# Weights of the second mixer split once, during the first; query and gate columns in one unit; softmax moved ahead of value sums

## The reference

```
# layer 1, mixer A (chunked gMLP), width 2048
h  = rms_norm(x, a_norm) * (1 + scale) + shift          # shift, scale, gate from c
u, v, z = split(h @ a_w_in)                             # (1024 x 6144)
v  = layer_norm(gelu(v)); mixed = per group lower-triangular 128x128 of v in chunks of 128
x  = x + gate * ((gelu(u) * mixed * silu(z)) @ a_w_out)
# shared keys and values
kv = rms_norm(x, kv_norm) @ w_kv;  k = rope(k)
# layer 2, mixer B (sliding window 128, 16 query heads, 2 key heads, sinks)
h  = rms_norm(x, b_norm) * (1 + scale) + shift
q, z = split(h @ b_w_in)                                # (1024 x 2048)
o  = softmax([q k^T / 8 masked, sink]) @ v              # blocks of 128 queries, 256 keys
x  = x + gate * ((o * silu(z)) @ b_w_out)
out = rms_norm(x, final_norm)
```

## Time and profile before

| | us |
|---|---|
| median of 3 runs | 2423.5 (2421.96 to 2425.0) |
| profiled execution, its own time | 2430.8 |
| its span, first to last instruction | 2429.0 |
| PE (matmul) busy in the span | 2274.2 (94%) |
| PE weight load busy | 1899.4 (78%) |
| DVE / POOL / ACT busy | 1314.8 / 1116.1 / 947.8 |
| granted TensorE clock, mean | 0.977 |
| moved by DMA | 375.73 MB, mean 155 GB/s |

### The profile page before, as it was taken

The page is one execution under the profiler, slowest core; times in us unless marked ns, Lnnn a source line. Parts: engine busy times, 40 slices in busy tenths (PEclk is TensorE's granted clock), DMA queues, the critical chain, the costliest instruction groups (busy, mean ns, idle before and its releaser), DMA issues.

```text
span 2429.0 us, 28242 instructions
## 1 busy us (share of the span) xinstructions
PE 2274.2 (94%) x10725; PEld 1899.4 (78%) x10725; DVE 1314.8 (54%) x1767; ACT 947.8 (39%) x1730; POOL 1116.1 (46%) x646
## 2 busy tenths in 40 slices
PE   3999999999999999999999999969789989998898
PEld 2787878888888888888888888857767877787786
DVE  5647891315744315644414554266577577657854
ACT  3223233433333433333423333344445545445553
POOL 3345554444444344444444443424544555564554
PEclk9999999999999999999999999989899999999999
DMA  7753334433434333344333346473634464573433
GB/s 278 268 202 114 128 130 165 165 97 120 147 113 169 128 119 117 121 144 156 121 104 105 122 140 224 134 251 102 237 106 159 176 239 132 187 256 130 156 113 113
DMA packets 188327, 375.73 MB, mean 155 GB/s; under 512 B 14272, under 2 KB 85024, under 8 KB 187552
## 3 DMA queue, kind: packets, MB, share of 16 engines
q1 hardware_dynamic: 185760, 368.65, 44.3%
q10 hardware_dynamic: 2432, 5.28, 0.6%
HBM read 295.23 MB, written 69.21 MB: 150 GB/s over the span
## 4 chain that ended last, share of the span: by engine, by line
PE 76%; DVE 10%; DMA 5%; DVEq 2%; issue 2%; ACT 2%; POOL 1%; SPq 1%; POOLq 0%; ACTq 0%
PE ps L1461 23%; PE ps L1463 23%; PE ps L1462 23%; PE ps L1611 2%; DMA w_raw<-in_a_w_out 1%; DMA r<-b_input 1%; PE ps L1649 1%; PE ps L1650 1%; POOL w_lo L704 1%; DVE wh L1305 1%; DVEq L1404 1%; DVE y_hl L1259 1%; DVE qs L1375 1%; DMA w_raw<-in_b_w_in 1%; PE ps L1673 1%
## 5 line engine op out<-in xcount | busy, mean ns | idle before, releaser
L704 POOL TENSOR_TENSOR w_lo<-w_raw,w_hi 128x1024 fp32r<-128x1024 f32 x360 | 900.9, 2513 | 991.1 <-ACT w_hi L814 990.7
L814 ACT ACTIVATE w_hi<-w_raw 128x1024 fp32r<-128x1024 f32 x360 | 380.3, 1061 | 822.6 <-DMA w_raw<-in_a_w_in 519.0
L1461 PE MATMUL ps<-h,w_hi 128*128 128x512 f32 x1024 | 402.3, 393 | 0.0
L1462 PE MATMUL ps<-h,w_hi 128*128 128x512 f32 x1024 | 398.9, 390 | 0.0
L1463 PE MATMUL ps<-h,w_lo 128*128 128x512 f32 x1024 | 398.8, 389 | 0.0
L1461 PE MATMUL ps<-r,w_hi 128*128 128x512 f32 x512 | 212.9, 416 | 26.8 <-DMA r<-b_input 11.3
L1463 PEld LDWEIGHTS ps<-h,w_lo 128*128 128x128 f32 x1024 | 192.5, 188 | 40.6
L1462 PEld LDWEIGHTS ps<-h,w_hi 128*128 128x128 f32 x1024 | 192.6, 188 | 39.5 <-issue 0.2
L1461 PEld LDWEIGHTS ps<-h,w_hi 128*128 128x128 f32 x1024 | 192.6, 188 | 39.2 <-POOL w_lo L704 0.2
L1462 PE MATMUL ps<-r,w_hi 128*128 128x512 f32 x512 | 206.1, 403 | 0.0
L1463 PE MATMUL ps<-r,w_lo 128*128 128x512 f32 x512 | 206.1, 402 | 0.0
(11 more groups left out here) (200 smaller groups left out, 4093.1 us busy)
## 6 DMA issues: line engine op xcount, KB each, us to landing
w_raw<-in_a_w_in SPq DMA_DIRECT2D x256, 256.0 KB, 3.0
w_raw<-in_a_w_in SPq DMA_DIRECT2D x64, 512.0 KB, 4.7
w_raw<-in_a_w_out SPq DMA_DIRECT2D x64, 512.0 KB, 4.1
w_raw<-in_b_w_in SPq DMA_DIRECT2D x64, 512.0 KB, 4.6
kv_input<-xks SPq DMA_DIRECT2D x32, 512.0 KB, 5.7
b_input<-hbs SPq DMA_DIRECT2D x32, 512.0 KB, 6.5
r<-b_input SPq DMA_DIRECT2D x16, 1024.0 KB, 10.9
w_raw<-b_out_gated SPq DMA_DIRECT2D x32, 512.0 KB, 4.2
```

The lines of the kernel that those rows point to most:

```text
L704: g.tensor_tensor(wlo[p][:, rows_], raw[p][:, rows_], whi[p][:, rows_].bitcast(F32), ALU.subtract).then_inc(w_lo, 1)
L814: s_.activation(whi[p][:, rows_], raw[p][:, rows_], ACT.Copy).then_inc(w_hi, 1)
L1461: t_.matmul(dst_, stat[0], mov[0], start=start, stop=False)
L1462: t_.matmul(dst_, stat[0], mov[1], start=False, stop=False)
```

## The change

- **Splitting.** The 13 distinct weight units of kv and B (26 halves, `SPLIT_UNITS`) are split once while A runs, in the stages `SPLIT_STAGES`: stages 6 to 10 of each group and 1, 2 of groups 1 to 3 (0 to 3 are value stages, 4 to 11 are u and z). In stage q SP loads the half into `wsr` ahead of the stage's odd unit; ACT copies it to `wsh` and POOL subtracts into `wsl` after the w_hi and w_lo of the next odd unit; SP stores both (512 KB each) to `b_weights_split` one stage later (`keep_split`). For the output weights (the last eight) DVE multiplies by the gate first; POOL's products L752 and their loads and stores go.
- **B's weights.** `b_half` loads `w_hi` and `w_lo` directly, two DMAs of 512 KB per half, and `hi` and `lo` are not called in B. PE waits for the landing.
- **Units of B.** q and z units are replaced by `qz` units of 256 query and 256 gate columns, n = 0 to 3. The order is kv, 8 qz units, 4 b units of the group before. Query tiles are in banks 0 and 1, gate tiles in 2 and 3.
- **Slots.** 6 before the first step, and 5 to 7 pieces in each step's slot.
- **Softmax order.** The gated output of step a is done by DVE in slot a + 2 after piece 0, behind that slot's softmax, instead of in slot a + 1 after piece 3. `oz_round` and `oz_rest` move behind piece 1 and 2.
- **First inputs.** Half of B's inputs of group 0 (`hb0`, 2 MB) are loaded into the place of `y_hl[0]` during A's last output units; PE waits for the quarters of `r` one by one.
- **Last group's tiles** use four banks, 4 to 7; the first logits wait for the sixth, the first transposes of probabilities for the eighth.

```diff
+    for i in range(NG):
+        units.append(("kv", i, 0, 0))
+        for n in range(4):
+            for ku in range(2):
+                units.append(("qz", i, n, ku))
         if i >= 1:
             for n in range(2):
                 for ku in range(2):
                     units.append(("b", i - 1, n, ku))
...
-PRO_SLOTS, STEPS, TAIL_SLOTS = 8, 16, 7
+PRO_SLOTS, STEPS, TAIL_SLOTS = 6, 16, 7
...
-    edges = [8 * n - 8 for n in B_STARTS[1:NG + 1]] + [8 * B_STARTS[NG + 1] + 4, B_PIECES]
+    edges = [30, 118, 208, 308, B_PIECES - 28, B_PIECES]
...
+SPLIT_UNITS = [("kv", 0, 0)] + [("qz", n, ku) for n in range(4) for ku in range(2)] \
+    + [("b", n, ku) for n in range(2) for ku in range(2)]
+SPLIT_STAGES = [(i, q) for i in range(NG) for q in ((1, 2) if i else ()) + (6, 7, 8, 9, 10)]
...
             def b_half(u, hh):
+                for m, w in ((0, whi[p]), (1, wlo[p])):
+                    sp.dma_start(w[:, 2 * hh:2 * hh + 2].bitcast(F32), wsd[split_of(u, hh), m]) \
+                        .then_inc(raw_in[2 * p + hh], 16)
...
+            def load_split(s):
+                if s >= 2:
+                    sp.wait_ge(split_out[m], 32 * (s // 2))
...
+            def keep_split(s):
+                sp.wait_ge(split_lo, s + 1)
+                sp.dma_start(wsd[s, 0], wsh[s % 2][:].bitcast(F32)).then_inc(split_out[s % 2], 16)
+                sp.dma_start(wsd[s, 1], wsl[s % 2][:].bitcast(F32)).then_inc(split_out[s % 2], 16)
+
+            def a_stage(i, q):
+                if q >= 1:
+                    unit(first + 2 * q)
+                s = split_at(i, q)
+                if s is not None:
+                    load_split(s)
+                if q >= 1:
+                    unit(first + 2 * q + 1)
+                s = split_at(i, q - 1)
+                if s is not None:
+                    keep_split(s)
...
                 for g in range(GROUPS + 1):
-                    unit(first + U_UZ + 2 * g)
-                    unit(first + U_UZ + 2 * g + 1)
+                    a_stage(i, 4 + g)
                     if i >= 1 and g >= 2:
                         keep_turned(i - 1, g - 2)
...
+            def split(i, q):                     # POOL; ACT has its like
+                pool.wait_ge(split_hi, s + 1)
+                g.tensor_tensor(wsl[m][:], wsr[m][:], wsh[m][:].bitcast(F32), ALU.subtract).then_inc(split_lo, 1)
...
                 for n in range(3, 10):
                     lo(first + n)
+                    if n % 2 == 1:
+                        split(i, (n - 3) // 2)
...
-                for u, hh in weights_at(pc):
-                    lo(u, (hh,))
...
-                    pe.wait_ge(w_lo, 2 * u + hh + 1)
+                    pe.wait_ge(raw_in[2 * (u % 2) + hh], landed(u))
...
-                        if 0 <= a - 2 < ATT and (a - 2) % 4 == 3:
-                            oz_rest(a - 2)
+                        if 0 <= a - 2 < ATT:
+                            gated_output(a - 2)
...
-                        x1_transposes(NG - 1, kt, 4 + kt % 2)
+                        x1_transposes(NG - 1, kt, 4 + kt % 4)
```

More of the change, by code:

```diff
@@ L43, in b_order @@
 def b_order():
[L46 to L50, removed]
+    units = []
+    for i in range(NG):
+        units.append(("kv", i, 0, 0))
+        for n in range(4):
             for ku in range(2):
[L52 to L60, removed]
+                units.append(("qz", i, n, ku))
         if i >= 1:
@@ L70, in b_order @@
             units.append(("b", NG - 1, n, ku))
-    return units, starts + [len(units)]
-B_UNITS, B_STARTS = b_order()
+    return units
+B_UNITS = b_order()
 B_AT = {unit: ub for ub, unit in enumerate(B_UNITS)}
@@ L121, in order, with split_at, splits_by, split_landed @@
     return (k % 4, k // 4) if by_halves(u) else (k // 2, k % 2)
[L124 to L134, removed]
+SPLIT_UNITS = [("kv", 0, 0)] + [("qz", n, ku) for n in range(4) for ku in range(2)] \
+    + [("b", n, ku) for n in range(2) for ku in range(2)]
+SPLITS = 2 * len(SPLIT_UNITS)
+SPLIT_STAGES = [(i, q) for i in range(NG) for q in ((1, 2) if i else ()) + (6, 7, 8, 9, 10)]
+FIRST_GATED = 2 * SPLIT_UNITS.index(("b", 0, 0))
+def split_at(i, q):
+    return SPLIT_STAGES.index((i, q)) if (i, q) in SPLIT_STAGES else None
+def splits_by(i, m):
+    return sum(1 for s, (g, _) in enumerate(SPLIT_STAGES) if g <= i and s % 2 == m)
+def split_landed(s):
+    return 16 * sum(2 if SPLIT_UNITS[t // 2][0] == "qz" else 1 for t in range(s % 2, s + 1, 2))
+def split_of(u, hh):
+    kind, g, n, ku = B_UNITS[u - FIRST_B]
+    return 2 * SPLIT_UNITS.index((kind, n, ku)) + hh
 def turned_at(pc):
     return (pc - 8) // 3 if pc >= 8 and pc % 3 == 2 and pc < 8 + 3 * KT else None
[L142 to L149 removed]
+def column_at(pc):
+    kind, g, n, ku, k = unit_of(pc)
+    if kind in ("qz", "b") and ku == 1:
+        if by_halves(FIRST_B + pc // 8):
+            return (kind, g, n, k - 4) if k >= 4 else (None, 0, 0, 0)
+        return (kind, g, n, k // 2) if k % 2 == 1 else (None, 0, 0, 0)
+    return None, 0, 0, 0
+def query_at(pc):
+    kind, g, n, j = column_at(pc)
+    return (g, 2 * n + j) if kind == "qz" and j < 2 else None
+def gate_at(pc):
+    kind, g, n, j = column_at(pc)
+    return (g, 2 * n + j - 2) if kind == "qz" and j >= 2 else None
+def gates_at(pc):
+    return [gate_at(last) for last in (pc - 1, pc) if gate_at(last) and (last % 8 == 7) == (last == pc)]
 def keys_in(s):
@@ L430, in landed @@
         def landed(u):
-            return 16 * sum(2 if w < FIRST_B and U_UZ <= w % A_UNITS < U_AO else 1 for w in range(u % 2, u + 1, 2))
+            return 16 * sum(2 if w >= FIRST_B or U_UZ <= w % A_UNITS < U_AO else 1 for w in range(u % 2, u + 1, 2))
         @block.sync
@@ L547, in _ @@
                 for j in range(4):
-                    if j >= 1:
-                        unit(first + 2 * j)
-                        unit(first + 2 * j + 1)
+                    a_stage(i, j)
                     if i == 0:
@@ L588, in _ @@
                             load_xk(0, part)
+                    if i == NG - 1 and n == 8:
+                        sp.wait_ge(piece_done, pieces(first + U_AO + 5, 8))
+                        sp.dma_start(hb0[:].bitcast(F32), hbd[0, 0:4].rearrange("k p a t -> p k a t")) \
+                            .then_inc(hb0_in, 16)
             for cnk in range(NC):
@@ L814, in hi, with split @@
                     s_.activation(whi[p][:, rows_], raw[p][:, rows_], ACT.Copy).then_inc(w_hi, 1)
+            def split(i, q):
+                s = split_at(i, q)
+                if s is None:
+                    return
+                m = s % 2
+                if s >= FIRST_GATED:
+                    act.wait_ge(split_gated, s + 1 - FIRST_GATED)
+                else:
+                    act.wait_ge(split_in[m], split_landed(s))
+                if s >= 2:
+                    act.wait_ge(split_out[m], 32 * (s // 2))
+                s_.activation(wsh[m][:], wsr[m][:], ACT.Copy).then_inc(split_hi, 1)
             def squares(src, total):
@@ new lines, in tasks @@
+                if kind == "b":
+                    dve.wait_ge(piece_done, b_pieces(pc + 1))
+                    if n == 0 and cnk == 0:
+                        dve.wait_ge(*((xr_in, 16 * (g + 1)) if g < NG - 1 else (xl_in, 32)))
+                    b, half = cnk + (4 if g == NG - 1 and n == 1 else 0), slice(512 * n, 512 * n + 512)
+                    dve.drain()
+                    v.tensor_tensor(xr_of(g, cnk)[:, half], xr_of(g, cnk)[:, half], bank(b), ALU.add) \
+                        .then_inc(bo_read, 1)
@@ L1717, in kv_piece @@
                 if kt % 4 == 0:
-                    pe.wait_ge(w_lo, 2 * u + kt // 4 + 1)
+                    pe.wait_ge(raw_in[2 * p + kt // 4], landed(u))
                 if kt in (0, 4, 6):
@@ L1754, in b_piece @@
                 else:
-                    piece = feature(u, ku, 0, r)
+                    piece = feature(u, ku, 0, hb0 if (g, n, ku) == (0, 0, 0) else r)
                 for m in range(2):
```

275 lines of the change are left out of this document (136 added, 139 removed).

## The result

The changed kernel takes 2455.72 us (median of 4 runs, 2451.71 to 2461.4); beside it on the same chip the kernel before took 2424.25 (2421.96 to 2426.44). The ratio is 1.0132, interval 1.0109 to 1.0155. The forecast was 2379.5 us, the range 2325 to 2430, and "slower" had a chance of 0.13. The profiled execution has a span of 2452.9 us, against 2429.0 before.

A forecast was written before the change was run, and what follows sets the result against it. PE bounds A, busy 1521 of 1585 us; in B 91 us of idleness and 42 us of reduced clock can be won. A loses 26, B gains 70: 2423.5 - 44 = 2379.5 us, range 2325 to 2430.

The forecast's parts named there:

- slower: Whole kernel: SP's wait costs 3.3 us or more in each of 21 stages, eating B's gain; at 4.5, 2448.5 us; chance 0.13.
- Step (5): Splitting in mixer A: late stores and even-unit loads on SP give 18 us of idleness, 26 lost with clock, bounds 0 and 50.
- The rival with the wait on SP: SP held in 21 stages makes the kernel slower; at 4.5 us each it costs 95, giving 2448.5 us; chance 0.13.
- Step (1): No splitting in mixer B: POOL, ACT and DVE relieved, so 39 of 48.8 us of waits ahead of the value sums go.
- The half about the masks: Mixer B: masks on POOL stand behind weight subtractions; without these, 10 of 48.8 us of value-sum waits stay.
- Step (4): Twice the weight traffic in mixer B: 310 GB/s, below 334, rope swaps queue behind; 10 us of new waits, bounds 0 and 25.
- Step (3): Prologue of mixer B: hb0 loaded early, but the last group's stores follow; 12 of 20 us of waits stay, gain 8.
- Step (2): Query and gate columns in one unit of mixer B: banks free earlier, 6 us of kvf, tt, r waits left, gain 11.
- The factor of 1.46 for the clock: Each us of PE idleness was taken to cost another 0.46 us of reduced clock, read from mixer B.
- B +70: Mixer B: 48 us less idleness plus 22 us of clock, a gain of 70 us, bounds 26 and 110.

The follow-up runs named there:

- Experiments 1: Changed kernel with the last keep_split of each group (stage 10) issued one stage later, behind stage 12's even unit; ratio 0.9887 to the kernel before.
- 3: Changed kernel with ACT's first y_round moved ahead of both the turned pair's rounding and the output unit's weight copy; ratio 0.9892 to the kernel before.
- 4: Kernel before with only SP's hold added ahead of the first output unit's loads, no splits made; ratio 1.0228 to the kernel before.
- experiment 5: Changed kernel with DVE's gated output back behind piece 3 of the next slot; ratio 0.9975 to the kernel before.
- experiment 7: Kernel before with only the gated output moved behind piece 0 two slots on, oz_round and oz_rest behind pieces 1 and 2; ratio 1.0006.
- experiment 10: Changed kernel with each group's last keep_split one stage later, gated output back, and B's rope swaps issued by ScalarE; ratio 0.9852 to the kernel before.
- experiment 8: Changed kernel with each group's last keep_split one stage later and the gated output back behind piece 3; ratio 0.9761 to the kernel before.

## Why the prediction was wrong

**Step (5), A loses 26: the mechanism was named, its victim was not.** The step said that keep_split holds SP, that the stored pair and the even unit come late behind it, and by how much: the stages show the split stored 13 to 14 us after the odd unit's load and the even unit loaded 16 to 17 us after it, and 13 to 16 was foreseen. Then it followed one thing to PE, the even unit's w_lo, in every stage. That was covered (8.9 us of waits for w_lo in the whole kernel, 6.6 before). It did not ask what else stands in ScalarE's order behind turned_round and w_hi. In the last group of each mixer-A stage that is y_round, in front of which DVE's y_rest waits, in front of the last mix's operands. Four waits of 10.5 to 14.8 us came instead of fifteen that counted 0.85 each and three of 1.7: 52.6 us of idle time for 18, and A lost 53.9 us, outside its own bounds of 0 and 50. Experiments 1, 3 and 4 fix it from three sides: take SP's hold away, take y_round out from behind it, or put the hold alone into the kernel before. The rival with the wait on SP had the place right (the queue) and the sign, and 2448.5 us was 7 us off, but its working (4.5 us in each of 21 stages) was as wrong as mine.

**Step (1), 39 us from the value sums: nothing came.** The first half held: no copy or subtraction of weights in B, the rope addition's mean 749 ns (1064 before). But I treated the new place of softmax and of the gated output as a gain alone ("it no longer waits there for ACT's copy"), and did not ask who waits for the gated output: the next value sums, for its bank. 48.9 us of waits took the place of 48.8. With the gate back (experiment 5) 25 of the 39 come. The half about the masks was right in the main, and hidden by the gate: in 19 of the changed kernel's 21 waits they are done 1.8 us or more ahead of the value sums, and alone they would leave some 17 us of waiting (an estimate from these times), where the forecast left 10.

**Step (4), 10 us for transfers: undersized.** DVE's waits for swaps went from 11.4 to 52.0 us. I had named the mechanism ("rope swaps queue behind them"), and priced it by mean rates: 310 GB/s fitted below 334. The mean hides it: the median landing of a swap hardly moved (2.0 to 2.3 us), the late ones are a few, with a latest of 10.3 us (5.6 before). Measured price: 38 us with the gate behind it, 24 without. The Trainium skill's figure of 358 GB/s (DMA: Bandwidth & Descriptors, "Specifications") does not bound these runs: 62 us moved 360 GB/s (1619.83 to 1682.11), and 10 us stretches moved up to 419. The kernel before already had such stretches (404 GB/s from 10 to 20 us, 414 from 1960 to 1970), so the prediction's "no stretch here reached 358" and its 334 as the fastest rate were read from windows too long. Neither figure says how late one 64 KB transfer lands.

**Step (3), the prologue: right.** From the first kv matmul to the first logits it is 62.3 instead of 74.2 us, with two pieces less in it. PE's idle time there falls from 20.3 to 10.1 us, a gain of 10 for the 8 forecast, and the DMA engines are busy at 0.97. **Step (2)** left its mark too: the waits for kvf, tt and r, 16.6 us without the first r, are 5.6, where 6 were left; but 5.2 us for gate tiles (zg) came, which the forecast did not have.

**The factor of 1.46 for the clock was too large.** In A 50.1 us of idle time cost 53.9; in B 22.8 less gave 30.0. It fitted only for the value-sum waits of experiment 5 (20.6 less idle, 30.7 shorter). One factor read from a whole mixer's clock gave 1.46 where 1.08 and 1.31 were measured. B's clock came to 0.96, where I had asked for 0.97.

In sum: A -26 became -53.9; B +70 became +30.0; together 24 us slower by the profiled executions, 32 by the medians.

## What to carry to other kernels

When a wait is put into one engine's queue, follow every instruction behind it, on each queue in turn, at each boundary of the loops and not in the typical stage: what was hit here was one rounding step that only the last group of a stage has. A store that nobody needs soon belongs behind the loads that somebody does; one stage later cost nothing and was worth 2.4%. And when a reordering moves work behind a transfer's wait, ask who waits for that work: its price can be paid back by what moved ahead (experiment 7), and be 38 us where that had nothing left to win.

## What was not expected of the hardware

A few small transfers landed very late. Swaps of 64 KB took up to 10.3 us on the queue of the bulk loads (5.6 before), at a median of 2.3. Issued by ScalarE, on another queue, they still took up to 7.6 at a median of 2.8 (experiment 10; 9.8 and 2.4 in experiment 8), so the shared queue is at most a part of it.

What DVE pays when it meets a subtraction on POOL hardly depends on its own size in these rows: a copy of 128x128 took 2.37 us instead of 0.21, an addition of 128x512 had taken 2.70 instead of 0.69. In proportion the small operations lose most.

After each of A's four gaps the granted clock was 1.2 GHz for another 3.9 to 6.1 us. The windows of the changed kernel after the third (it ends at 1133.54):

```profile
1133.00:1135.00 2.00, 1.46 (x7) 1.46 (x8) 1.92 (x4) 0.00 (x0) 0.00 (x0) 0.50 0.00 0
1135.00:1137.00 2.00, 2.00 (x11) 2.00 (x11) 1.93 (x4) 0.00 (x0) 0.00 (x0) 0.50 0.17 70
1137.00:1139.00 2.00, 2.00 (x11) 1.81 (x11) 1.82 (x3) 0.00 (x0) 0.00 (x0) 0.73 1.00 395
1139.00:1141.00 2.00, 2.00 (x10) 1.66 (x9) 1.91 (x3) 0.87 (x2) 0.00 (x0) 1.00 0.90 234
```

Here 1.2 GHz ends about 4.5 us after work resumes, so the clock costs some 2 us (an estimate: half of that) for a gap of 13.9. The mean clock of 0.67 inside the gap (1119.60 to 1133.54) costs nothing, since PE has no work there.
